# Token statistics on narrow columns and a mean subtracted on GpSimd: one change to the layer norms of a fused decoder layer

## The reference

```python
def layer_norm(x, g, b):
    mu = jnp.mean(xf, axis=-1, keepdims=True)
    var = jnp.mean(jnp.square(xf - mu), axis=-1, keepdims=True)
    y = (xf - mu) * lax.rsqrt(var + LN_EPS) * g + b
def trunk_layer(x, ...):
    q, k, v, iq, ik, iw, p = split_proj(x, w_in)           # 2048 -> 3656
    a = attend(...)          # indexer scores all keys, top-k kept, attention over those
    m = pooling over trailing 2/4/8/16 tokens, a linear map per group
    mix = einsum(concat([a, m]), w_out)                      # 2048 -> 2048
    x = layer_norm(DEEPNORM_ALPHA * x + mix, ln1_g, ln1_b)   # the first norm
    f, conv_state = conv_ffn(x, conv_prefix, w_up, conv_w, conv_b, w_down)
    x = layer_norm(DEEPNORM_ALPHA * x + f, ln2_g, ln2_b)     # the second norm
def conv_ffn(x, u_prefix, w_up, conv_w, conv_b, w_down):
    u = einsum(x, w_up)                                      # 2048 -> 2 * 5632
    c = conv_b + sum over j of conv_w[j] * u_ext[:, j:j+Q]   # width 3, causal
    h = silu(gate) * val                                     # the two halves of c
    return einsum(h, w_down), u_ext[:, -2:]                  # 5632 -> 2048
```

## Time and profile before

| | us |
|---|---|
| median of 3 runs | 1461.3 (1459.06 to 1462.87) |
| the profiled execution | 1457.07 |
| its span, first to last instruction | 1455.4 |
| PE busy | 1366.0 (94%) |
| VectorE / ScalarE / GpSimd busy | 777.1 / 602.8 / 112.5 |
| mean granted TensorE clock | 0.977 |

### The profile page before, as it was taken

One profiled execution on the slowest core, in us unless ns is written; L12 is line 12 of the kernel. 1 busy time (PEld: TensorE's weight loads), 2 busy tenths in 40 slices (PEclk: granted clock), 3 DMA queues, 4 the chain that ended last, 5 costly groups with the idle time before them and its releaser, 6 DMA issues.

```text
span 1455.4 us, 25489 instructions
## 1 busy us (share of the span) xinstructions
PE 1366.0 (94%) x9772; PEld 1235.0 (85%) x9772; DVE 777.1 (53%) x1294; ACT 602.8 (41%) x964; POOL 112.5 (8%) x197
## 2 busy tenths in 40 slices
PE   6999998889999995899999999999999999999994
PEld 6968676558543794899999999999999999999993
DVE  4546785674321357556556565655656544543435
ACT  4333222225222236445455554545545433333334
POOL 5510000000000000001001010000101310000000
PEclk9999999989999998899999999999999999999997
DMA  8655988985699640555555555555555655555551
GB/s 252 188 156 175 329 294 289 273 293 186 199 319 303 192 144 22 194 163 157 174 160 173 162 161 172 158 174 162 163 171 154 192 169 150 169 159 157 162 159 66
DMA packets 101213, 272.70 MB, mean 187 GB/s; under 512 B 13177, under 2 KB 19650, under 8 KB 100706
## 3 DMA queue, kind: packets, MB, share of 16 engines
q1 hardware_dynamic: 98530, 268.43, 59.6%
q0 software_dynamic: 2560, 2.63, 0.7%
HBM read 265.83 MB, written 5.18 MB: 186 GB/s over the span
## 4 chain that ended last, share of the span: by engine, by line
PE 76%; SPq 8%; DVE 6%; DMA 5%; issue 4%; ACT 1%; DVEq 0%
PE G L432 23%; PE G L433 23%; PE G L434 23%; SPq L275 3%; SPq L313 2%; DMA k_ring<-in_kT_cache 2%; SPq L365 2%; PE A L582 1%; PE A L729 1%; DVE z L1648 1%; DVE w_lo L1280 1%; DMA raw<-in_w_out 1%; DVE z L1647 1%; SPq L339 1%; SPq L294 1%
## 5 line engine op out<-in xcount | busy, mean ns | idle before, releaser
L1280 DVE TENSOR_TENSOR w_lo<-raw,w_hi 128x1024 fp32r<-128x1024 f32 x354 | 432.9, 1223 | 478.0 <-ACT w_hi L958 476.8
L958 ACT ACTIVATE w_hi<-raw 128x1024 fp32r<-128x1024 f32 x354 | 373.9, 1056 | 576.9 <-PE G L434 470.6
L432 PE MATMUL G<-x_hi,w_hi 128*128 128x290 f32 (+1 forms) x1856 | 561.7, 303 | 36.8 <-DVE w_lo L1280 27.4
L433 PE MATMUL G<-x_lo,w_hi 128*128 128x290 f32 (+1 forms) x1856 | 555.4, 299 | 0.0
L434 PE MATMUL G<-x_hi,w_lo 128*128 128x290 f32 (+1 forms) x1856 | 551.8, 297 | 0.0
L432 PEld LDWEIGHTS G<-x_hi,w_hi 128*128 128x128 f32 x1856 | 352.9, 190 | 47.9 <-issue 34.2
L433 PEld LDWEIGHTS G<-x_lo,w_hi 128*128 128x128 f32 x1856 | 354.5, 191 | 0.2
L434 PEld LDWEIGHTS G<-x_hi,w_lo 128*128 128x128 f32 x1856 | 352.1, 190 | 0.0
L433 PE MATMUL G<-h_lo,w_hi 128*128 128x288 f32 x704 | 209.9, 298 | 0.0
L434 PE MATMUL G<-h_hi,w_lo 128*128 128x288 f32 x704 | 209.1, 297 | 0.0
L432 PE MATMUL G<-h_hi,w_hi 128*128 128x288 f32 x704 | 208.5, 296 | 0.0
(11 more groups left out here) (281 smaller groups left out, 1123.4 us busy)
## 6 DMA issues: line engine op xcount, KB each, us to landing
raw<-in_w_up SPq DMA_DIRECT2D x176, 512.0 KB, 3.6
raw<-in_w_down SPq DMA_DIRECT2D x88, 512.0 KB, 3.6
k_ring<-in_kT_cache SPq DMA_DIRECT2D x128, 256.0 KB, 4.3
raw<-in_w_in SPq DMA_DIRECT2D x48, 512.0 KB, 5.2
v_ring_x<-in_v_cache SPq DMA_DIRECT2D x80, 256.0 KB, 4.0
raw<-in_w_out SPq DMA_DIRECT2D x32, 512.0 KB, 3.8
v_ring_p<-in_v_cache SPq DMA_DIRECT2D x48, 256.0 KB, 4.2
raw<-in_w_iq SPq DMA_DIRECT2D x8, 512.0 KB, 6.7
```

Of the source, the lines that this page charges most:

```text
L432: pe.matmul(out, hi, xh, start=start, stop=False)
L433: pe.matmul(out, hi, xl, start=False, stop=False)
L958: act.activation(w_hi[:, c, 0:width], raw[:, c, 0:width], ACT.Copy).then_inc(hi_done, 1)
L1280: dve.tensor_tensor(w_lo[:, c, 0:width], raw[:, c, 0:width], w_hi[:, c, 0:width].bitcast(f32), ALU.subtract).then_inc(lo_done, 1)
```

## The change

It has these parts:

1. `SUMS`: in the first norm, PE's sums of groups 0, 1 and 2 stand after chunks 82, 85 and 88, instead of after 84, 88 and 89. The sums of a group wait for each block by itself.
2. Token statistics. PE also totals the partial sums with the partial sums as weights and one column of ones as moving operand: three pieces of 128 tokens give three columns, with a token per partition, for the mean and three for the squares. The wide matmul stays for the mean only. Variance, root and reciprocal are formed on these three columns (`ln_s`). The reciprocal is copied to 3 x 128 columns, and three matmuls against the identity spread it over all partitions in bank 1 of `A`. VectorE multiplies the blocks by that bank.
3. `CENTRE`: GpSimd subtracts the mean from blocks 2 to 15 of the first norm and from the odd blocks of the second. VectorE waits for `centred` and multiplies.
4. The splits of chunks 93 to 98 stand between the norm's blocks: on ScalarE after the odd blocks from 5 on, on VectorE at the even blocks from 6 on.
5. SyncE loads chunks 93 to 97 ahead of its wait for `x1_lo`; convolution parameters and state follow, then chunk 98. ScalarE waits for these two only after emptying slab 0.
6. A one-column root after the squares of group 2 has the root's table loaded there, in both norms.
7. The output is stored in pairs of blocks.

```diff
+CENTRE = (range(2, KB), range(1, KB, 2))
+SUMS = {(2, 0): 0, (2, 3): 1, (3, 2): 2}
+        def spread_rows(tmp):
+            return tmp[:, 1:3].rearrange("p a n -> p (a n)")[:, 0:384].rearrange("p (i c) -> p i c", c=128)
 # SyncE
+            for n in range(UP0 + RING, UP0 + 8):
+                load_chunk(n)
             sp.wait_ge(x1_lo, KB)
...
-            for n in range(UP0 + RING, DN0 + 8):
+            for n in range(UP0 + 8, DN0 + 8):
...
-            for k in range(KB):
-                sp.wait_ge(normed, KB + k + 1)
-                sp.dma_start(yT[:, k, META:T], z2[:, k, :]).then_inc(rows_out, 16)
+            for k in range(0, KB, 2):
+                sp.wait_ge(normed, KB + k + 2)
+                sp.dma_start(yT[:, k:k + 2, META:T], z2[:, k:k + 2, :]).then_inc(rows_out, 16)
 # TensorE: sums
                 for q in range(4):
+                    if g:
+                        pe.wait_ge(g_free, 4 * (slab + g) + q + 1)
 # TensorE: totals
-                pe.wait_ge(part_kept, 2 * round_ + 1)
-                pe.matmul(A[:, 3, 0:n], ones[:], tmp[:, 3, :], start=True, stop=True).then_inc(total_mm, 1)
-                pe.wait_ge(part_kept, 2 * round_ + 2)
-                pe.matmul(A[:, 0, 0:n], ones[:], tmp[:, 4, :], start=True, stop=True).then_inc(total_mm, 1)
+                starts = (0, 128, n - 128)
+                for a in range(2):
+                    pe.wait_ge(part_kept, 2 * round_ + a + 1)
+                    for i, t0 in enumerate(starts):
+                        mm = pe.matmul(A[:, 0, 4 * a + i:4 * a + i + 1], tmp[:, 3 + a, t0:t0 + 128], ones[:, 0:1],
+                                       start=True, stop=True)
+                    if a == 0:
+                        mm = pe.matmul(A[:, 3, 0:n], ones[:], tmp[:, 3, :], start=True, stop=True)
+                    mm.then_inc(total_mm, 1)
+                pe.wait_ge(rstd_kept, round_ + 1)
+                for i, t0 in enumerate((0, 128, 256)):
+                    m = min(128, n - t0)
+                    mm = pe.matmul(A[:, 1, t0:t0 + m], spread_rows(tmp)[:, i, :], ident[:, 128 - m:128], start=True, stop=True)
+                mm.then_inc(rstd_mm, 1)
 # GpSimd, called for z1 ahead of its wait for x1_lo, and for z2 after the residual
+            def centre(z, tmp, blocks, round_):
+                pool.wait_ge(mean_kept, round_ + 1)
+                for k in blocks:
+                    pool.tensor_tensor(z[:, k], z[:, k], tmp[:, 0], ALU.subtract).then_inc(centred, 1)
 # ScalarE: norm
-                act.activation(tmp[:, 1], A[:, 3, 0:n], ACT.Square, scale=1.0 / (32 * D)).then_inc(sq_mean, 1)
+                act.activation(tmp[:, 0], A[:, 3, 0:n], ACT.Copy, scale=1.0 / (32 * D)).then_inc(mean_kept, 1)
                 act.wait_ge(var_done, round_ + 1)
-                act.activation(tmp[:, 1], tmp[:, 2], ACT.Sqrt, bias=tiny[:, 15:16]).then_inc(sd_done, 1)
+                act.activation(ln_s[:, 6:9], ln_s[:, 3:6], ACT.Sqrt, bias=tiny[:, 15:16]).then_inc(sd_done, 1)
...
+                        if k >= 5 and k % 2:
+                            hi(UP0 + k // 2 + 1)
 # ScalarE: around it
-                if f == AO + 9:
-                    squares(z1q, ln_a, 0, SL_A, 0)
+                if f in (AO + 6, AO + 9, AO + 13):
+                    squares(z1q, ln_a, (f - AO - 5) // 4, SL_A, 0)
...
+                    act.activation(tiny[:, 14:15], tiny[:, 15:16], ACT.Sqrt)
...
-            for n in range(UP0 + RING, UP0 + 6):
-                hi(n)
-            act.wait_ge(conv_in, 32)
...
-                for n in range(UP0 + 8 * i + 6, UP0 + 8 * i + 10):
+                for n in range(UP0 + 8 * i + (6 if i else 9), UP0 + 8 * i + 10):
 # VectorE: norm
-                dve.scalar_tensor_tensor(out=tmp[:, 2], in0=A[:, 0, 0:n], scalar=1.0 / (32 * D), in1=tmp[:, 1],
+                then(dve.tensor_scalar(ln_s[:, 0:3], A[:, 0, 0:3], 1.0 / (32 * D), None, ALU.mult))
+                then(dve.tensor_tensor(ln_s[:, 3:6], ln_s[:, 0:3], ln_s[:, 0:3], ALU.mult))
+                dve.scalar_tensor_tensor(out=ln_s[:, 3:6], in0=A[:, 0, 4:7], scalar=1.0 / (32 * D), in1=ln_s[:, 3:6],
                                          op0=ALU.mult, op1=ALU.subtract).then_inc(var_done, 1)
-                then(dve.tensor_scalar(tmp[:, 0], A[:, 3, 0:n], 1.0 / (32 * D), None, ALU.mult))
+                dve.wait_ge(mean_kept, round_ + 1)
                 for k in range(2):
-                    then(dve.tensor_tensor(z[:, k], z[:, k], tmp[:, 0], ALU.subtract))
+                    if k not in blocks:
+                        then(dve.tensor_tensor(z[:, k], z[:, k], tmp[:, 0], ALU.subtract))
                 dve.wait_ge(sd_done, round_ + 1)
-                then(dve.reciprocal(tmp[:, 2], tmp[:, 1]))
+                then(dve.reciprocal(ln_s[:, 9:12], ln_s[:, 6:9]))
+                dve.tensor_copy(spread_rows(tmp), ln_s[:, 9:12].unsqueeze(2).to_broadcast([128, 3, 128])).then_inc(rstd_kept, 1)
+                dve.wait_ge(rstd_mm, round_ + 1)
                 for k in range(KB + 1):
                     if k < KB:
-                        if k >= 2:
+                        if k in blocks:
+                            dve.wait_ge(centred, len(CENTRE[0]) * round_ + blocks.index(k) + 1)
+                        elif k >= 2:
                             then(dve.tensor_tensor(z[:, k], z[:, k], tmp[:, 0], ALU.subtract))
-                        dve.tensor_tensor(z[:, k], z[:, k], tmp[:, 2], ALU.mult).then_inc(scaled, 1)
+                        dve.tensor_tensor(z[:, k], z[:, k], A[:, 1, 0:n], ALU.mult).then_inc(scaled, 1)
...
+                        if k >= 6 and k % 2 == 0:
+                            lo(UP0 + k // 2)
```

More of the change, by code:

```diff
@@ L137, in layer @@
     sel_sb = put("sel_sb", [128, 2, TS])
+    ln_s = put("ln_s", [128, 12])
     wsel = put("wsel", [128, 2, TS])
@@ L252, in layer @@
         squared, part_mm, part_kept, total_mm = sem("squared"), sem("part_mm"), sem("part_kept"), sem("total_mm")
-        sq_mean, var_done, sd_done, scaled, normed, x1_hi, x1_lo = (
-            sem("sq_mean"), sem("var_done"), sem("sd_done"), sem("scaled"), sem("normed"), sem("x1_hi"), sem("x1_lo"))
+        mean_kept, var_done, sd_done, rstd_kept, rstd_mm = (
+            sem("mean_kept"), sem("var_done"), sem("sd_done"), sem("rstd_kept"), sem("rstd_mm"))
+        centred, scaled, normed, x1_hi, x1_lo = (
+            sem("centred"), sem("scaled"), sem("normed"), sem("x1_hi"), sem("x1_lo"))
         ctx_put, tail_put, conv_a, conv_v, silu_done, gated_done = (
@@ L833, in sums @@
                 n = z.shape[2]
-                if g:
-                    pe.wait_ge(g_free, 4 * (slab + g) + 4)
-                else:
+                if g == 0:
                     pe.wait_ge(shifted, 4 * round_ + 4)
@@ L860, in _ @@
                         shift_sum(z1q, SL_A, 0)
-                    if s >= 2 and c == 2:
-                        sums(z1q, ln_a, s - 2, SL_A, 0)
-            sums(z1q, ln_a, 2, SL_A, 0)
+                    if (s, c) in SUMS:
+                        sums(z1q, ln_a, SUMS[s, c], SL_A, 0)
             sums(z1q, ln_a, 3, SL_A, 0)
@@ L942, in _ @@
                                    ALU.add).then_inc(residual, 1)
+            centre(z2, ln_b, CENTRE[1], 1)
         @block.scalar
@@ L1197, in _ @@
                     keep_shift(ln_a, 0)
-                if f == AO + 9:
-                    squares(z1q, ln_a, 0, SL_A, 0)
+                if f in (AO + 6, AO + 9, AO + 13):
+                    squares(z1q, ln_a, (f - AO - 5) // 4, SL_A, 0)
                 if f == AO + 13:
-                    squares(z1q, ln_a, 1, SL_A, 0)
-                if f == AO + 15:
-                    squares(z1q, ln_a, 2, SL_A, 0)
+                    act.activation(tiny[:, 14:15], tiny[:, 15:16], ACT.Sqrt)
             hi(UP0 + 2)
@@ L1223, in _ @@
                                    G[:, j, PT:NQ].rearrange("p (b q) -> p b q", q=DQ), ACT.Copy).then_inc(g_free, 1)
+                if i == 0:
+                    act.wait_ge(conv_in, 32)
                 for c in range(10, 14):
@@ L1679, in _ @@
             dve.wait_ge(g_free, 4 * SL_UP)
-            norm(z1q, ln_a, 0, True)
-            for n in range(UP0 + RING, UP0 + 6):
-                lo(n)
+            norm(z1q, ln_a, CENTRE[0], 0, True)
             for i in range(NUP):
@@ L1690, in tap @@
                                                     op0=ALU.mult, op1=ALU.add)
-                for c in range(6, 10):
+                for c in range(6 if i else 9, 10):
                     lo(UP0 + 8 * i + c)
@@ L1748, in _ @@
             dve.wait_ge(g_free, 4 * (SL_DN + NDN))
-            norm(z2, ln_b, 1, False)
+            norm(z2, ln_b, CENTRE[1], 1, False)
 def constants():
```

6 lines of the change are left out of this document (3 added, 3 removed).

## The result

The changed kernel takes 1452.37 us (median of 11 runs, 1445.36 to 1457.46), the kernel before 1461.11 on the same chip (11 runs, 1456.23 to 1462.87). The ratio is 0.994 (0.9921 to 0.996): faster by 8.7 us, by the interval 5.8 to 11.5. The forecast was 1454.1.

What follows compares the result with a forecast made beforehand. TensorE, busy 94% of the span, bounds the kernel, so gains lie where it stands still. 6.1 us up to chunk 98 plus 1.1 in the second norm make 7.2: 1461.3 to 1454.1 us, range 1446 to 1460.5.

Steps and rivals of the forecast that it cites:

- Sums: First norm: group 2's sums ahead of chunk 89 leave ScalarE's split bare, loss 1.1 us; the two earlier groups 0.
- Statistics: First norm, first total to first multiply: 5.5 us against 5.27, hand-overs eating the fast reciprocal and root; plus 0.2.
- at the low clock: First norm's three spreading matmuls with both hand-overs: taken 1.05 us, range 0.8 to 1.8 if at the low clock.
- Shared port: First norm: GpSimd and VectorE shut each other out; four VectorE operations wait 0.4 us each, 1.6 (0 to 3.2).
- 1.2 or more named as a sign: Sign the forecast is right: GpSimd subtractions in two lengths, 0.8 and 1.2 us or more.
- Ring: Splits between first norm's blocks: 3.8 us per block pair against PE's 3.2, PE hardly affected, 14.4 us hole gone.
- What is late next: Chunk 98, loaded behind last x_lo, parameters and state: PE stands 5.8 us, low clock costs 1.9; gain 6.1.
- Second norm: Tail: first multiply 0.8 us late, loop 11.3 instead of 13.55, last store loses 0.4; gain 1.1.
- the free port: Rival 1: the shared port costs nothing, 1450.4 us, or 1445.5 if the ring keeps PE's 3.2; chance 23%.
- the table loads: Rival 2, both norms: squares need another table, 1.28 us paid twice per norm, 5.1 in all, 1459.2 us; chance 9%.
- VectorE did not wait for all of GpSimd: Rival 3, both norms: everything on VectorE waits for GpSimd, eighteen operations cost 20 us, total 1470, slower; chance 7%.
- the ring at 4.8 us: Rival 4, first norm: the hole only moves; 4.8 us per pair, chunk 98 5 us later, 1459 us; chance 9%.

Runs made afterwards that it cites:

- the kernel with splits alone: Kernel before plus only the early loads of chunks 93 to 97, splits of 93 to 98 between norm blocks, later wait for convolution loads: ratio 0.997, 1456.37 us.
- The earlier loads: Changed kernel with chunks 98 to 100 also loaded ahead of SyncE's wait for the last x_lo: ratio 0.987 to the kernel before, median 1442.79 us.

## Why the prediction was right, step by step

The forecast of 7.2 us is within the interval, and the mechanisms that it counted come to just that. From the common event: chunk 98 starts 7.9 us sooner (77.24 against 85.1), the low clock behind the new stand costs 2.2 (chunk 98 to w_down's end takes 828.96 in the kernel with splits alone, 826.8 before), the tail gives 1.5: 7.2, and in the second run of the changed kernel, 0.6 later at chunk 98, 6.5. But from the common event to the end the changed kernel gained 10.9 in its first profile and 10.2 in its second. The rest is w_down's pace, 3.9 us, of which the prediction had no word. That 1454.1 still came so near the median is in part luck: a term of half the gain was missing, and the medians (8.7, interval 5.8 to 11.5) do not resolve it.

1. **Sums.** Predicted 1.1, measured 1.2 for the sums of group 2; all of the part costs 1.6 (31.3 against 29.7). The other 0.4 is the step's one wrong term: it put the earlier places of groups 0 and 1 at nothing on a full PE, but the squares of group 0 delay a split, and PE stands before chunk 82.
2. **Statistics.** Predicted +0.2, measured +0.43 (11.20 without GpSimd against 10.77 before). The spreading matmuls alone took 1.50, where 1.05 was counted with both hand-overs: the case "at the low clock" of its range came true.
3. **Shared port.** Predicted 1.6, measured 1.13. Three of the four operations waited as forecast, 0.22 and 0.77 for both subtractions; the copy did not wait, and the first x_lo blocks did instead. GpSimd's own operations never stood still for a whole one: 1.01 at most, not the 1.2 or more named as a sign. Its price was read from the longest case of the earlier trace rows; the changed kernel's residual adds have the same one, 1.81 us. The port's rule by the Trainium skill ("SBUF — State Buffer", section "SBUF: two separate sides") puts an exclusive lock on VectorE operations with two SBUF inputs, and on copies of fp32 within SBUF too. For the first the trace agrees that the two delay each other; for the copy, 0.55 with and without GpSimd, VectorE's side of it is not seen, and the measurement decides. Chunk 90 was forecast 43.4 us behind the common event and came at 43.6. The near hit is made of errors that cancel: 0.5 and 0.2 too little in steps 1 and 2, 0.5 too much here.
4. **Ring.** 3.8 us per pair forecast, 3.72 measured; PE ran through to chunk 98, as said.
5. **What is late next.** From the common event the last x_lo ended at 68.35 (68.2 forecast), and chunk 98 started at 77.24 (77.2) after a stand of 5.4 us (5.8), at clock 0.50. The earlier loads show the cause. One reading of the prediction is off by 0.1: before the change, chunk 98 started at 605.9, ahead of the emptying of slab 0's last tile at 606.12.
6. **Second norm.** Predicted 1.1, measured 1.5. The first multiply came 1.0 late from w_down's end (0.8 forecast), and the loop made up for it: VectorE's subtractions in it took 0.45 after the first (0.85), so the 0.9 set aside for GpSimd was mostly not spent.

Of the rivals, the free port falls with the kernel without GpSimd; the table loads did not come back (four in the trace, and the squares ran behind the root's); VectorE did not wait for all of GpSimd (two multiplies still take 0.82); the ring at 4.8 us did not occur. The fourth rival's idea, that the hole moves, holds in part: 5.4 of 14.4 us came back in another place.

What was missing is a term no step had: a new tile shifts all behind it, and that changed PE's pace over 285 us. It added half of what the mechanisms gave.

## What to carry to other kernels

When a stall is removed, look first at the order of one queue: here five early issues of SyncE made the gain in the first norm, and three more brought as much again. The interleaving gave nothing with five and, by the estimate above, is needed for what the three more bring: what a part is worth depends on which wait ends last. The narrow columns gave nothing in the first norm. Before a gain is put down to an edit, compare the pace of stretches that the edit doesn't touch; if a new tile stands ahead of the operands, run the old kernel with an empty one in its place. GpSimd as a helper pays where VectorE is the bound (2.4 us in the tail, 1.6 to 1.9 at the last x_lo), and costs where VectorE is on a short serial path (1.1 us).

## What the hardware showed

- TensorE's pace depends on where its operands lie in SBUF: 131.3 or 133.1 ns per matmul of 288 columns, at granted clock 1.00 in both, by 64 bytes of shift. The difference is in the products h_lo x w_hi (292 or 298 ns each).
- Between GpSimd and VectorE the delay goes both ways. In the norms it was smaller than a whole operation: a subtraction of 290 columns on GpSimd took between 0.69 and 0.92 us; on VectorE 0.47 alone, 0.85 beside GpSimd, 0.95 at worst. Operations with one input in PSUM and one in SBUF were not slowed (0.82 for two multiplications with and without GpSimd). The longest delay was that of one residual add, 1.81 instead of 0.81.
- A subtraction of 290 columns takes GpSimd 0.69 us, one of 288 columns 0.79. Tile and place differ too, so the cause is open.
- A stand of 3.36 us was followed by granted clock 0.50, one of 2.38 us by 1.00, for the same six matmuls (1.50 and 0.86 us).
